# Experts' gate and up products with the weights loaded and 96-slot token blocks streamed, in a two-layer decoder trunk

## The reference

```
def _swiglu(h, wg, wu, wd):
    return (jax.nn.silu(h @ wg) * (h @ wu)) @ wd

def _moe(h, router, wg, wu, wd):
    ...
    top_v, top_i = lax.top_k(logits, TOP_K)
    gates = jax.nn.softmax(top_v, axis=-1)
    combine = jnp.einsum('blk,blke->ble', gates, jax.nn.one_hot(top_i, N_EXPERTS, dtype=f32))
    y = jnp.zeros(h.shape, f32)
    for e in range(N_EXPERTS):
        y = y + combine[..., e:e + 1] * _swiglu(h, wg[e], wu[e], wd[e]).astype(f32)
    return y.astype(h.dtype)
```

## Time and profile before

| | |
|---|---|
| Time, median of 3 runs | 1634.34 us (1631.61 to 1641.16) |
| Time of the profiled execution | 1637.31 us |
| Its span | 1634.3 us |
| Mean granted TensorE clock | 0.987 |
| Busy: PE, PEld, DVE, ACT | 1590.1, 1309.2, 1137.9, 896.8 us |

### The profile page before, as it was taken

One profiled execution on the slowest core, in us unless ns is written; L12 is line 12 of the kernel. 1 busy time (PEld: TensorE's weight loads), 2 busy tenths in 40 slices (PEclk: granted clock), 3 DMA queues, 4 the chain that ended last, 5 costly groups with the idle time before them and its releaser, 6 DMA issues.

```text
span 1634.3 us, 27320 instructions
## 1 busy us (share of the span) xinstructions
PE 1590.1 (97%) x10856; PEld 1309.2 (80%) x10856; DVE 1137.9 (70%) x1476; ACT 896.8 (55%) x1190; POOL 123.3 (8%) x180
## 2 busy tenths in 40 slices
PE   9999999999999999899999999999999999999999
PEld 7766687999998777778767878888787887878787
DVE  4663741677766753335468889797988979798897
ACT  3362541544325353343436777676777767687774
POOL 1104000000000003220222000000000000000100
PEclk9999889999999999998999999999999999999999
DMA  8923533544423240000449999797989979798993
GB/s 334 407 94 124 207 130 123 220 187 170 175 81 119 103 155 1 3 3 2 187 165 395 380 376 412 316 427 305 425 350 376 409 312 426 303 425 347 384 423 121
DMA packets 41103, 404.74 MB, mean 248 GB/s; under 512 B 4784, under 2 KB 5072, under 8 KB 11664
## 3 DMA queue, kind: packets, MB, share of 16 engines
q1 hardware_dynamic: 34336, 372.25, 56.6%
q0 software_dynamic: 6672, 31.14, 4.7%
HBM read 379.09 MB, written 26.30 MB: 248 GB/s over the span
## 4 chain that ended last, share of the span: by engine, by line
PE 88%; DVE 5%; ACT 2%; DMA 2%; issue 2%; POOL 0%; DVEq 0%; ACTq 0%; SPq 0%; POOLq 0%
PE ps L2342 85%; DMA ring<-in_moe_w 1%; PE ps L3127 1%; DMA arena<-in_moe_w 1%; DVE rest_ring L2149 1%; PE ps L2809 1%; PE ps L2750 1%; DVE arena L1688 0%; ACT arena L1270 0%; DVE arena L1701 0%; ACT arena L1283 0%; PE ps L3080 0%; PE ps L2544 0%; DVE h L2057 0%; DVE arena L1776 0%
## 5 line engine op out<-in xcount | busy, mean ns | idle before, releaser
L2342 PE MATMUL ps<-head,hsel 128*128 128x512 f32 x1408 | 457.5, 396 | 2.8 <-DVE rest_ring L2149 2.8
L2342 PEld LDWEIGHTS ps<-head,hsel 128*128 128x128 f32 x1408 | 264.3, 188 | 61.5 <-DVE rest_ring L2149 7.8
L2149 DVE TENSOR_TENSOR rest_ring<-ring,head 128x2048 fp32r<-128x2048 f32 x128 | 291.0, 2284 | 14.4 <-ACT head L1423 14.3
L2342 PE MATMUL ps<-arena,ring 128*128 128x288 f32 (+9 forms) x1408 | 256.6, 347 | 1.3 <-ACT arena L1276 1.2
L1423 ACT ACTIVATE head<-ring 128x2048 fp32r<-128x2048 f32 x128 | 243.1, 1912 | 24.9 <-DMA ring<-in_moe_w 24.9
L2342 PEld LDWEIGHTS ps<-arena,ring 128*128 128x128 f32 (+4 forms) x1408 | 199.5, 189 | 53.1 <-issue 7.7
L2342 PE MATMUL ps<-rest_ring,hsel 128*128 128x512 f32 x512 | 199.6, 390 | 0.0
L2342 PE MATMUL ps<-head,actT_split 128*128 128x512 f32 x512 | 169.1, 394 | 9.0 <-issue 6.3
L2342 PE MATMUL ps<-rest_arena,head 128*128 128x288 f32 x704 | 174.8, 296 | 0.0
L2342 PE MATMUL ps<-rest_arena,rest_ring 128*128 128x288 f32 x528 | 155.5, 294 | 0.0
L2342 PE MATMUL ps<-h,ring 128*128 128x288 f32 (+2 forms) x624 | 133.6, 370 | 3.7 <-ACT h L1332 1.9
(11 more groups left out here) (387 smaller groups left out, 2283.1 us busy)
## 6 DMA issues: line engine op xcount, KB each, us to landing
ring<-in_moe_w SPq DMA_DIRECT2D x64, 2048.0 KB, 12.4
ring<-in_moe_w SPq DMA_DIRECT2D x64, 1024.0 KB, 8.3
arena<-in_moe_w SPq DMA_DIRECT2D x24, 2048.0 KB, 11.6
arena<-in_moe_w SPq DMA_DIRECT2D x24, 1024.0 KB, 6.6
ring<-in_ffn_w SPq DMA_DIRECT2D x11, 2048.0 KB, 7.4
ring<-in_ffn_w SPq DMA_DIRECT2D x11, 1024.0 KB, 4.8
moe_rows<-arena POOLq DMA_DIRECT2D x1, 6656.0 KB, 34.0
ring<-in_w_in SPq DMA_DIRECT2D x2, 3072.0 KB, 12.8
```

The lines of the kernel that those rows point to most:

```text
L2149: V.tensor_tensor(mrest[s][:, o:o + w], mslot[s][:, o:o + w], mhead[c % 2][:, o:o + w].bitcast(F32), ALU.subtract).then_inc(sem("gu_split" ...
L2342: return nc.tensor.matmul(o, l, r, start=start, stop=stop, skip_group_check=skip)
```

## The change

The operands of gate and up change places. The weights become stationary, 128 columns at a time, and the tokens move, 96 slots. A slice k has four blocks of 128 weight columns (two of gate, two of up), and each has three products, so `up(c)` issues 8 x 4 x 3 = 96 matmuls of 96 columns in place of 24 of 512. The result comes out in the layout that `down` needs, 128 hidden columns by slots, so `turn` and its two transposes are gone, with what ACT and DVE read from their bank: ACT rounds `actm` from SBUF (`act_head`), DVE takes the rest from SBUF (`act_rest`). `down` has the same 12 matmuls, with 96 stationary columns. The blocks have 96 slots, up to 13 jobs could exist (`NE + 5`), the rows in DRAM are laid out for 96, and the transposes of tokens are 96 wide. Banks are dealt out anew (two for a chunk's gate and up). POOL's reading and writing of rows is put in the loop by chunks, and ACT and DVE take the weight pieces at a job's start and end in a slightly different order.

```
-        DOWN_BANKS = [0, 1, 2, 7, 5, 6, 3, 4]
+        GU_BANKS, DOWN, TOKB = (0, 2), 4, 6
...
+            def act_head(j, c):
+
+                act.wait_ge(sem("gu_free"), FC * j + c + 3)
+                if c >= 2:
+                    act.wait_ge(sem(f"dn_slot_free{(c - 2) % MS}"), uses[(c - 2) % MS] * j + (c - 2) // MS + 2)
+                A(actTm[c % 2][0], actm[c % 2], ACT.Copy).then_inc(sem("moe_act_head"), 1)
...
+            def act_products(j, first, c):
+
+                dve.wait_ge(sem("silu_ready"), FC * j + c + 1)
+                if c >= 2 or not first:
+                    dve.wait_ge(sem("moe_act_rest"), FC * j + c - (1 if c else 0))
+                V.tensor_tensor(actm[c % 2], sgm[c % 2], gu_banks(c)[:, 1], ALU.mult).then_inc(sem("gu_free"), 1)
+
+            def act_rest(j, c):
+
+                dve.wait_ge(sem("moe_act_head"), FC * j + c + 1)
+                V.tensor_tensor(actTm[c % 2][1], actm[c % 2], actTm[c % 2][0].bitcast(F32), ALU.subtract)\
+                    .then_inc(sem("moe_act_rest"), 1)
...
                 def up(c):
 
                     s = c % MS
-                    pe.wait_ge(sem("gu_free"), FC * j + c + 1)
+                    pe.wait_ge(sem("gu_free"), FC * j + c + (1 if c else 2))
                     wh, wr = (t[:, 0:GU].rearrange("p (k n) -> p k n", k=KT) for t in (mhead[c % 2], mrest[s]))
-                    hh, hr = hsel
+                    sums = gu_banks(c)
...
-                        mm(ps[:, c % 2, :], hh[:, k, :], wh[:, k, :], k == 0, False)
-                        mm(ps[:, c % 2, :], hh[:, k, :], wr[:, k, :], False, False)
-                        ins = mm(ps[:, c % 2, :], hr[:, k, :], wh[:, k, :], False, k == KT - 1)
+                        for i in range(4):
+                            cols_ = slice(i * P, (i + 1) * P)
+                            o = sums[:, i // 2, (i % 2) * SL:(i % 2 + 1) * SL]
+                            mm(o, wh[:, k, cols_], hsel[:, k, 0, :], k == 0 and i % 2 == 0, False, skip=True)
+                            mm(o, wr[:, k, cols_], hsel[:, k, 0, :], False, False, skip=True)
+                            ins = mm(o, wh[:, k, cols_], hsel[:, k, 1, :], False, k == KT - 1, skip=True)
                     ins.then_inc(sem("gu_full"), 1)
-
-                def turn(c):
-
-                    pe.wait_ge(sem("gu_free"), FC * j + c + 3)
-                    pe.wait_ge(sem("tr_free"), FC * j + c + (1 if c else 2))
-                    for u in range(2):
-                        ins = nc.tensor.transpose(turned(c)[:, u * P:(u + 1) * P], actm[c % 2][:, u * P:(u + 1) * P], ident)
-                    ins.then_inc(sem("tr_full"), 1)
```

## The result

Median 2741.31 us of 4 runs (2737.50 to 2749.41), against 1633.47 us of 4 runs before (1631.61 to 1641.16): a ratio of 1.678, with a 95% interval of 1.672 to 1.684. The forecast was 2060 us, at most 2600. The direction was right; the time lies outside the range.

A forecast was written before the change was run, and what follows sets the result against it. PE's distance between matmul starts was taken to bound the expert stage. Profiled 1637 us + 436 for `up`'s loads - 10 for late starts = 2063, median 3 us lower, so 2060 us; range 1930 to 2600.

The forecast's parts named there:

- PE's clock 1.00: Expert stage: PE was expected to run at its full 2.4 GHz after the change.
- the third rival: Expert stage: PE's clock falls to 1.2 GHz, 3240 us if throughout, from 2200 if partly; chance 0.13, half under 2600.
- The step per matmul: `up`: each 96-column matmul takes 0.111 us, set by loading 128 stationary columns; 10.66 us per chunk.
- The fixed part: `up`: a fixed 0.014 us per matmul that might come on top of the load, making the step 0.125 us.
- the four passes: `up`: narrow fp32r runs like fp32, 0.160 us a step (2480 us) or 0.222 (3000 us); chance 0.15.
- the cheap load: `up`: fp32r load no longer than the stream, 0.054 us a step, 1590 us; chance 0.04.
- `down`: Expert stage: its 12 matmuls still move 512 columns at 0.227 us each, 2.72 us per chunk as before.
- DVE, ACT and the weights: Expert stage: DVE's 7.7 us, ACT's 6.5 and the weights' 8.4 per chunk stay hidden under PE's 13.4.
- The ends of jobs: Between jobs: half of PE's 2.1 us of late starts per job goes, -10 us over the kernel.
- the forecast's case: Whole kernel: load-bound step at full clock, 2060 us; 2000 to 2250 us given 0.60.

The follow-up runs named there:

- e10: The change (96 slots) with PE's loop over jobs 1 to 6 written out, without a jump back: 2681.27 us.
- e9: The change with 112 slots in place of 96 and PE's loop over jobs 1 to 6 written out, without a jump back: 2102.73 us.
- e1: The change with blocks of 128 slots in place of 96, so 128 columns streamed per load: 2295.61 us.
- e8: The change with blocks of 112 slots in place of 96, PE's loop over jobs kept: 2305.68 us.
- e3: The change with each block of 96 token columns streamed twice in `up`, 192 columns per load, the second copy unread: 2119.72 us.
- e2: The change with only 64 of each 128 weight columns loaded in `up`, half of gate and up left out: 1676.96 us.

## Why the prediction was wrong

**The step that failed is the clock.** "PE's clock 1.00" in the stage was assumed, and falling in part or all of it was the third rival, at 0.13. It came true: half clock for three quarters of the stage. The rival had its price right ("a part of it, anything from 2200 on") and its reason too: loads of many columns for short streams, with no gap. I gave it little because the streams there had 8 and 16 columns; between those and the 288 of elsewhere the trace of before has, beside full loads, only short groups such as the eight of the earlier trace rows. So it left open what 96 columns would do, and it might as well have gone one way as the other. Beside this `down` the clock fell at 96 (the change and e10) and, behind the first job, held at 112 (e9). The 17 per cent that separate them decide over some 580 us: 2681 in e10, 2103 in e9.

**The step per matmul was right.** 0.111 forecast, 0.1117 measured, at 96, 112, 128 and 192 columns; 0.213 at half clock; 0.0584 with half the load. The fixed part does not come on top (the forecast's 0.014 for it was a slip: 0.227 less 512 x 0.00042 leaves 0.012), and neither the four passes nor the cheap load came about. The Trainium skill's sustained figure of about 81 ns at 128 columns (TensorE: Matmul & The Clock Gate, Back-to-back issue gap) is below the 0.1117 us that e1 shows there.

**`down`** kept 0.227 us a step at full clock. **DVE, ACT and the weights** stayed hidden: 274 and 231 us busy of 800, 150 GB/s.

**The ends of jobs** were booked at -10 us. The jumps, which the forecast did not have, cost +24 us of idling, and 55 in all in the change; in e8, where the clock hangs on them, 182.

**The sum.** With a full clock the forecast's case was 2060; e9, with 112 slots, and e3, with 192 columns and its gaps, took 2103 and 2120. From 2060 to 2741 there are then 43 us of small terms, some 580 of clock falls without a gap (e10 less e9), and 60 between e10 and the change, nearly all of the jumps. The small terms are a job that takes 151.1 - 95.8 = 55.3 us more than before where the forecast had (436 - 10) / 8 = 53.2, some 16 in eight jobs, and about 30 lost in the 61 us at half clock of the first. The range reached to 2600 on the strength of four passes and of half of the clock rival; it would have had to hold that rival whole.

## What to carry to other kernels

Before making a weight load the partner of a short stream, price the step by the load (0.1117 us for 128 columns here), and then ask what clock it will run at: count the stretches of the trace in which the clock fell with PE full, and if the new shape lies between those and the ones where it held, give both cases real chances. Keep long streams together in a block and near every restart rather than spread among short ones; the same matmuls took 2741 and 3096 us. And look at the first instruction after a loop's jump back: 5.4 us of idle time there cost e8 36 us each time, because the clock fell behind it.

## What was unexpected of the hardware

- With the same number of matmuls and the same loads in `up`, streaming more columns is faster: 2741 us at 96, 2306 at 112, 2296 at 128, 2120 at 192 (of the last three, most of the difference is how soon the clock returns behind the gaps).
- Behind a gap of 4.9 to 5.8 us the half clock lasts until the next `down` at 112 and 128 columns (61 us and more), but under 7 us at 192 (behind 5.4 to 6.9 us of idling). Seven gaps of 1.50 us in e9 changed nothing; an eighth, of 1.64 us, had 3.4 us at half behind it.
- A loop's jump back leaves TensorE idle for 2.2 to 5.0 us with 76 matmuls per chunk in its body, 2.9 to 6.9 with 108, and not at all with 38. Why is open.
- At 96 columns the granted clock falls with PE full when each load has 128 columns, and stays at full between chunks when it has 64 (e2).
